# Rotary pairs fetched by four small DMA copies per tile, and a layer loop written out, in a two-layer streaming encoder

## The chip, the cores and the metric

One core of one Trainium2 chip runs the whole step. The metric is the device time of one execution in microseconds (us); of several runs the median is given. TensorE multiplies matrices, VectorE and ScalarE work elementwise, GpSimd (POOL) copies, fills and issues DMAs from its own queue, SyncE (SP) issues the weight DMAs.

## The reference

Two request groups (528 prompt frames with 16 meta tokens, 64 running frames, together 592) go through two layers. What touches the change, per layer:

```python
proj = rmsnorm(x, norm1_g) @ w_in
q, k, v, ... = split(proj)            # 16 query heads, 2 key/value heads of 64
q = partial_rotary(q, pos); k = partial_rotary(k, pos)

def partial_rotary(x, pos):           # ROT_DIM 16, half 8
    x1, x2 = x[..., :8], x[..., 8:16]
    return concat([x1*cos - x2*sin, x2*cos + x1*sin, x[..., 16:]])
```

Then follow sliding-window attention, a short convolution branch, a Conformer branch with a convolution of width 31, a gated merge with the output projection, and a ConvFFN. After the second layer comes a final RMSNorm.

## The kernel before

Data lie channel-major: 128 channels on the partitions, 592 frames (TOK) along the free axis, so the 1024 channels are eight tiles and a tile holds two query heads. A weight panel is 128 output channels by 1024 inputs; 174 panels (PANELS) per layer pass through two buffers. For a panel in buffer s, SP loads raw weights (L310), ScalarE makes the high part (`step`, L732), VectorE the low part (`step`, `low`, L982), and TensorE does 8 x 3 x 2 = 48 matmuls of 128x296 (`panel`, L424): high by high, high by low, low by high, two halves of the frames. When a panel is done, both `step`s prepare the panel after next.

The order of work on each engine is written out by hand, one program per engine, with semaphores between them; each engine takes its instructions in that order. Layers are a hardware loop with a register, `Fori(0, DEPTH)`, on GpSimd (L326), TensorE (L595), ScalarE (L776) and VectorE (L1066); inside a layer there are smaller hardware loops.

The Q stage works so. TensorE runs the K panel (L641), then eight Q panels (`queries`, L630), then V (L647). ScalarE copies each result from PSUM into one of two slots of a scratch area (K: L808, Q: L814, V: L817; the slots are O_QR). For the rotation TensorE multiplies the copied tile by a permutation matrix with signs (`rotate`, L612 with the matmul in L616, one Q panel later), and VectorE forms tile x cos (L1146), sin x product (L1148) and their sum (L1150). For the keys TensorE makes four such products (`keys`, L620, L626): each of the two key heads, plain and permuted, written to both halves of the partitions; VectorE multiplies them by cos and sin (L1135) and adds (L1138, L1139) into KD, which has each key head on both halves. Between the rotations VectorE works off convolution taps of the Conformer branch (`taps`, L1029; `first_taps`, L1017), and a `step` per panel. After the last rotation it does six taps, the step of V, and then the first score maxima of attention (L1188). GpSimd copies the rotated queries of a chunk into a padded staging area (`stage`, L345, L358, L359), for the first key head once four rotations are done, for the second once all eight are; TensorE's first scores (L499) need that, the copied V and the keys.

At the layer's turn TensorE begins with blocks of the first two panels (`two_panels`, L450), then a channel sum (L460); ScalarE takes the root (L751 loads the table, L753), VectorE the reciprocal (L1000).

Of the kernel before, what the change touches and what calls it, by code (L numbers as in the profile page):

```python
# [66 lines left out]
D_CF, D_K, D_Q, D_V, D_OA, D_SC, D_OS, D_OC, D_WO, D_FF, ND = 0, 8, 12, 20, 22, 30, 46, 54, 62, 70, 116  # L67
# [15 lines left out]
PIECES = ((0, 0, HALF, 0), (1, 0, TP - HALF, HALF), (1, TP - HALF, DEC_SEQ, TP))  # L83
# [68 lines left out]
def encoder(nc, weights, xt, vecs, consts, kcache, vcache, cfhist, spill, y, kp, vp, scp, cfp, ffp, ks, vs):  # L152
# [24 lines left out]
    nsink = sb("neg_sink", [128, DEPTH * 8])  # L177

# [48 lines left out]


# [26 lines left out]
    qrot_ps, krot_ps = sem("qrot_ps"), sem("krot_ps")  # L255
# [63 lines left out]
    def _(pool):  # L319
# [6 lines left out]
        with pool.Fori(0, DEPTH) as l:  # L326
# [16 lines left out]
            plain()  # L343

            def stage(c, n):  # L345
# [66 lines left out]
    def _(pe):  # L412
        def panel(w, s, out, nk, rh, rl, kwait=None, k0=0, k1=KT, between=None):

            pe.wait_ge(lo_done, w + 1)
            for k in range(k0, min(nk, k1)):
                if between and k == 2:
                    between()
# [3 lines left out]
                for j, (a, b) in enumerate(((wh, rh), (wh, rl), (wl, rh))):  # L422
                    for h in range(2):
                        last = nc.tensor.matmul(out[:, h, :], a[:, s, wk], b[:, k, h * HALF:(h + 1) * HALF],  # L424
                                                start=(k == 0 and j == 0), stop=(k == nk - 1 and j == 2))
# [3 lines left out]
        def two_panels(w, outs, nk, r0, r1, free, kwait, last_late, middle=None):  # L429
# [7 lines left out]
            order += [(p, k) for p in range(2) for k in range(nk - 3, nk)]  # L437
            for u, (p, k) in enumerate(order):
# [9 lines left out]
                for j, (a, b) in enumerate(((wh, rh), (wh, rl), (wl, rh))):  # L448
                    for h in range(2):
                        last = nc.tensor.matmul(outs[p][:, h, :], a[:, p, wk], b[:, k, h * HALF:(h + 1) * HALF],  # L450
# [17 lines left out]
        def residual(l, w, d, nk, rh, rl, kwait):  # L468

            two_panels(l * PANELS + w, (d_tile(d), d_tile(d + 1)), nk, (rh, rl), (rh, rl),  # L470
                       [(d_out, d_free(l, d + j)) for j in range(2)], kwait, True)
            with pe.Fori(1, 4) as i:
                for j in range(2):
                    pe.wait_ge(d_out, l * ND + i * 2 + (d + j + 1))
                    panel(l * PANELS + i * 2 + (w + j), j, d_tile(d + j), nk, rh, rl)

        def first_pair(l, w, a, d, kwait, last_late, middle=None):

            two_panels(w, (a_tile(a), d_tile(d)), KT, (xh, xl), (xh, xl), ((a_out, a_free(l, a)), (d_out, d_free(l, d))),
                       kwait, last_late, middle)  # L480

        def pair(l, w, a, d, rg, ro, kwait=None, middle=None):

            pe.wait_ge(a_out, a_free(l, a[0]))
            panel(w, 0, a_tile(a[1]), KT, *rg)
# [3 lines left out]
            panel(w + 1, 1, d_tile(d[1]), KT, *ro, kwait=kwait)  # L489
# [80 lines left out]
        def attention_end(l):  # L570
# [3 lines left out]
            def gate_part(k0, k1):  # L574
                panel(l * PANELS + P_OA, 0, a_tile(A_OA), KT, xh, xl, k0=k0, k1=k1)
# [19 lines left out]
        with pe.Fori(0, DEPTH) as l:  # L595
# [7 lines left out]
            def glu(i, j):  # L603
                pair(l, W + i * 4 + (P_CF + 2 * j), (i * 2 + (A_CF + j), A_CF + j), (i * 2 + (D_CF + j), D_CF + j),
                     (xh, xl), (xh, xl))
            first_pair(l, W + P_CF, A_CF, D_CF, (nx_lo, l * 24), False, mean_square1)
            first_pair(l, W + P_CF + 2, A_CF + 1, D_CF + 1, (nx_lo, l * 24 + 8), False)
# [4 lines left out]
            def rotate(i, j):  # L612
                pe.wait_ge(a_out, l * NA + i * 2 + (A_Q + j + 3))
                pe.wait_ge(d_out, l * ND + i * 2 + (D_Q + j + 1))
                for h in range(2):
                    last = nc.tensor.matmul(d_tile(D_Q + j)[:, h, :], con[:, CON["rot"]:CON["rot"] + 128],  # L616
                                            slot(O_QR, TOK, j)[:, h * HALF:(h + 1) * HALF], start=True, stop=True)
                last.then_inc(qrot_ps, 1)

            def keys():  # L620

                pe.wait_ge(a_out, a_ready(l, A_K))
                for j, name in enumerate(("ka", "kar", "kb", "kbr")):
                    pe.wait_ge(d_out, d_free(l, D_K + j))
# [974 lines left out]
```

## Time and profile before

| | |
|---|---|
| three runs | 2595.13, 2599.48, 2603.38 us, median 2599.48 |
| profiled execution | span 2596.4 us from the first to the last instruction; no other time of its own is given |
| TensorE (PE), weight loads (PEld) | busy 2533.4 us, 2493.8 us |
| VectorE, ScalarE, GpSimd | busy 1649.4, 865.6, 74.3 us |

Busy time is the union of an engine's instructions. Matmuls overlap in the records, so one lasts about 300 ns while a pair starts every 270 ns; the pace is read from starts. An idle time in square brackets names what ended it; "issue" means that nothing the profile shows was waited for.

### The profile page before, as it was taken

To read this page: it belongs to the slowest core of one execution; us is meant where nothing else is said; L and a number is where in the kernel's file an instruction comes from. 1 tells how busy PE (TensorE), PEld (TensorE's weight loads), DVE (VectorE), ACT (ScalarE), POOL (GpSimd) and SP (SyncE) were. 2 spreads that over 40 slices of the span, in tenths; PEclk is the share of its full clock that TensorE was granted. 3 is DMA by queue.
4 is the path that set the end of the run, shared out by engine and by line. 5 is a ranking of instruction groups with operands and counts; after the bars stand their busy time and mean duration, and the time that the engine had idled before them with its cause. 6 is when DMAs were issued, how large, how long until landed. Compare 5 with 4: busy or idle time off the path is not lost.

```text
span 2596.4 us, 49209 instructions
## 1 busy us (share of the span) xinstructions
PE 2533.4 (98%) x17938; PEld 2493.8 (96%) x17938; DVE 1649.4 (64%) x2468; ACT 865.6 (33%) x1624; POOL 74.3 (3%) x133
## 2 busy tenths in 40 slices
PE   6999999999999999999999999999999999999997
PEld 6998899999999999999999988999999999999996
DVE  8768667776534663645777775777755356546367
ACT  4124422223523442423432143322235234324244
POOL 0002100000000000000000021000000000000000
PEclk9998899999999999999999979999999999999998
DMA  4220012222233222222232100222222322222222
GB/s 180 81 65 25 8 65 81 80 77 79 82 105 95 75 80 81 81 81 81 94 106 81 65 9 8 81 82 81 81 74 87 104 91 82 78 79 79 81 81 104
DMA packets 55331, 203.13 MB, mean 78 GB/s; under 512 B 6606, under 2 KB 6670, under 8 KB 54958
## 3 DMA queue, kind: packets, MB, share of 16 engines
q1 hardware_dynamic: 52560, 190.03, 22.3%
q0 software_dynamic: 2656, 11.57, 1.5%
q8 instruction: 72, 1.18, 0.2%
q14 instruction: 43, 0.35, 0.0%
HBM read 193.14 MB, written 8.50 MB: 78 GB/s over the span
## 4 chain that ended last, share of the span: by engine, by line
PE 93%; DVE 3%; issue 2%; ACT 1%; DVEq 0%; DMA 0%; ACTq 0%; SPq 0%
PE ps L424 79%; PE ps L450 5%; PE ps L535 4%; PE ps L499 2%; PE ps L514 1%; PE ps L516 1%; DVE w_lo L982 1%; DVE cf_acc L1029 1%; ACT w_hi L732 0%; PE ps L547 0%; PE ps L460 0%; PE ps L616 0%; DVE scratch L996 0%; DVE x_q_merged L1458 0%; DMA vec<-in_vecs 0%
## 5 line engine op out<-in xcount | busy, mean ns | idle before, releaser
L424 PE MATMUL ps<-xn_hi,w_hi 128*128 128x296 f32 x3584 | 786.3, 301 | 4.8 <-DVE w_lo L982 4.7
L424 PE MATMUL ps<-xn_hi,w_lo 128*128 128x296 f32 x3584 | 781.5, 299 | 0.0
L424 PE MATMUL ps<-xn_lo,w_hi 128*128 128x296 f32 x3584 | 779.6, 299 | 0.0
L982 DVE TENSOR_TENSOR w_lo<-raw,w_hi 128x1024 fp32r<-128x1024 f32 x350 | 429.1, 1226 | 540.3 <-ACT w_hi L732 538.1
L732 ACT ACTIVATE w_hi<-raw 128x1024 fp32r<-128x1024 f32 x348 | 369.0, 1060 | 1205.9 <-PE ps L424 1141.2
L424 PEld LDWEIGHTS ps<-xn_hi,w_hi 128*128 128x128 f32 x3584 | 583.9, 189 | 8.0 <-DVE w_lo L982 5.8
L424 PEld LDWEIGHTS ps<-xn_lo,w_hi 128*128 128x128 f32 x3584 | 583.5, 189 | 0.0
L424 PEld LDWEIGHTS ps<-xn_hi,w_lo 128*128 128x128 f32 x3584 | 581.0, 188 | 0.0
L1029 DVE SCALAR_TENSOR_TENSOR cf_acc<-glu,vec,cf_acc 128x622 f32<-128x622 f32 x368 | 295.7, 862 | 0.1
L424 PE MATMUL ps<-branch_hi,w_hi 128*128 128x296 f32 x1296 | 284.0, 300 | 0.3
L424 PE MATMUL ps<-branch_hi,w_lo 128*128 128x296 f32 x1296 | 282.3, 299 | 0.0
L424 PE MATMUL ps<-branch_lo,w_hi 128*128 128x296 f32 x1296 | 281.6, 299 | 0.0
L424 PEld LDWEIGHTS ps<-branch_hi,w_hi 128*128 128x128 f32 x1296 | 210.6, 188 | 2.3 <-DVE w_lo L982 1.7
L424 PEld LDWEIGHTS ps<-branch_lo,w_hi 128*128 128x128 f32 x1296 | 210.8, 189 | 0.0
L424 PEld LDWEIGHTS ps<-branch_hi,w_lo 128*128 128x128 f32 x1296 | 209.8, 188 | 0.0
L1404 DVE SCALAR_TENSOR_TENSOR scratch<-scratch,vec 128x594 f32<-128x594 f32 x176 | 147.2, 837 | 54.4 <-ACT scratch L943 45.7
L943 ACT ACTIVATE scratch<-scratch,vec 128x594 f32<-128x594 f32 x88 | 69.9, 795 | 164.2 <-DVE scratch L1427 99.5
L1450 DVE TENSOR_TENSOR x_q_merged<-x_q_merged,ps 128x592 f32 x48 | 37.0, 771 | 128.3 <-PE ps L424 118.4
L1017 DVE SCALAR_TENSOR_TENSOR cf_acc<-glu,vec,cf_acc (+1 forms) x112 | 97.1, 867 | 27.5 <-DVE cf_acc L1017 20.5
L535 PEld LDWEIGHTS ps<-scratch 128*128 128x128 f32 (+3 forms) x576 | 89.6, 197 | 19.6 <-DVE scratch L1204 3.6
L535 PE MATMUL ps<-scratch 128*128 128x64 f32 (+5 forms) x576 | 105.0, 300 | 2.6 <-DVE scratch L1204 2.6
L499 PE MATMUL ps<-scratch 128*128 (+4 forms) x320 | 72.9, 387 | 7.4 <-ACT scratch L828 5.1
(159 smaller groups left out, 2325.0 us busy)
## 6 DMA issues: line engine op xcount, KB each, us to landing
raw<-in_weights SPq DMA_DIRECT2D x350, 512.0 KB, 3.3
spill<-x_q_merged POOLq DMA_DIRECT2D x2, 2368.0 KB, 9.7
x_q_merged<-spill POOLq DMA_DIRECT2D x16, 296.0 KB, 3.1
x_q_merged<-in_xt SPq DMA_DIRECT2D x4, 592.0 KB, 8.2
out_y<-x_q_merged SPq DMA_DIRECT2D x8, 296.0 KB, 2.3
con<-in_consts SPq DMA_DIRECT2D x1, 592.0 KB, 11.3
vec<-in_vecs SPq DMA_DIRECT2D x1, 576.0 KB, 5.7
out_cfp<-glu POOLq DMA_DIRECT2D x4, 120.0 KB, 5.6
```

The lines of the kernel that those rows point to most:

```text
L424: last = nc.tensor.matmul(out[:, h, :], a[:, s, wk], b[:, k, h * HALF:(h + 1) * HALF], start=(k == 0 and j == 0), stop=(k == nk - 1 and j ...
L450: last = nc.tensor.matmul(outs[p][:, h, :], a[:, p, wk], b[:, k, h * HALF:(h + 1) * HALF], start=(k == 0 and j == 0), stop=(k == nk - 1 an ...
L499: last = nc.tensor.matmul(PS[:, 2 * v + i // 2, 256 * (i % 2):256 * (i % 2) + nk], view(O_QS + 512 * v + 128 * i, 128), keys, start=True, ...
L514: last = nc.tensor.transpose(PS[0:n1, 4, 128 * i:128 * i + 128], P[:, 0:n1], ident)
L535: last = nc.tensor.matmul(PS[:, 6, 64 * i:64 * i + 64], scr[0:nn, o + 512 * v + 128 * i:o + 512 * v + 128 * i + 128], vals, start=(i == 0 ...
L732: nc.scalar.activation(wh[:, s, :], raw[:, s, :], ACT.Copy).then_inc(hi_done, 1)
L943: nc.scalar.activation(dst, src[:, 0:S_OUT], ACT.Identity, bias=0.0, scale=col(l, "ffw", m * 3)) \
L982: return V.tensor_tensor(wl[:, s, :], raw[:, s, :], f(wh[:, s, :]), ALU.subtract).then_inc(lo_done, 1)
L1017: V.scalar_tensor_tensor(tile(acc, m), src, col(l, "cfw", m * CF_K + k), tile(acc, m), ALU.mult, ALU.add).then_inc(tap_glu, 1)
L1029: V.scalar_tensor_tensor(a, tile(G, 2 * g + t, k, CF_OUT), col(l, "cfw", k + (2 * g + t) * CF_K), a, ALU.mult, ALU.add).then_inc(tap_rest[ ...
L1404: V.scalar_tensor_tensor(dst, src[:, k:k + S_OUT], col(l, "ffw", m * 3 + k), dst, ALU.mult, ALU.add) \
L1450: V.tensor_tensor(halves(tile(X, m)), halves(tile(X, m)), d_tile(d0 + n + j), ALU.add) \
```

## The change

- Rotation without TensorE: `rotate` and `keys` go, with their PSUM places. GpSimd issues four DMA copies per tile inside the scratch area (`partners`): for each of the two heads of a tile rows 8 to 15 to the place of rows 0 to 7, and back (8 rows of 592 floats each). VectorE multiplies by a sine whose sign is set once, in layer 0. The other partner rows are zeroed once per layer by GpSimd.
- Keys: K is rotated once, 128 partitions, as a tile; VectorE then writes the sum of each head to both halves.
- The copied K goes to slot 1 instead of 0; copies and issues wait for the rotation two tiles back.
- The layer loop is written out on the four engines: the layer number is a constant.
- The first kept frame of a layer becomes a function, `first(l)`, which is 0 for both layers; `kept`, `kept_tile`, `half(l)` and `pieces(first(l))` stand where the whole tile, HALF and PIECES stood (these many lines are left out below). After the last layer the casts for a next layer are left out.

```diff
+ROT_IN = 4 * 16
...
+KEEP0 = (0, 0)
+def first(l):
+    return KEEP0[min(l, DEPTH - 1)]
+def half(l):
+    return (TOK - first(l)) // 2
...
 @block.gpsimd
-        with pool.Fori(0, DEPTH) as l:
+        for l in range(DEPTH):
...
+            pool.wait_ge(glu_first, l + 1)
+            nc.gpsimd.memset(view(O_TQ, 2 * TOK), 0.0).then_inc(rot_zero, 1)
+            pool.wait_ge(rot_zero, l + 1)
+            def partners(s):
+                for h in (0, HEAD_DIM):
+                    x1, x2 = slice(h, h + ROT // 2), slice(h + ROT // 2, h + ROT)
+                    pool.dma_start(slot(O_TQ, TOK, s)[x1, :], slot(O_QR, TOK, s)[x2, :]).then_inc(rot_in[s], 16)
+                    pool.dma_start(slot(O_TQ, TOK, s)[x2, :], slot(O_QR, TOK, s)[x1, :]).then_inc(rot_in[s], 16)
+            pool.wait_ge(a_out, a_ready(l, A_K))
+            partners(1)
+            for m in range(KT):
+                pool.wait_ge(a_out, a_ready(l, A_Q + m))
+                pool.wait_ge(qrot, l * KT + m + 1)
+                if m == 1:
+                    pool.wait_ge(krot, l * 2 + 2)
+                partners(m % 2)
             def stage(c, n):
-                        pool.wait_ge(qrot, l * KT + 4 * (v + 1))
+                        pool.wait_ge(qrot, l * KT + (4 * (v + 1) + 2))
...
 @block.tensor
-        with pe.Fori(0, DEPTH) as l:
+        for l in range(DEPTH):
...
-            def rotate(i, j):
...
-            def keys():
...
                     panel(W + i * 2 + (P_Q + j), 1 - j, a_tile(A_Q + j, half(l)), KT, xh, xl)
-                    if j:
-                        rotate(i, 0)
-                    elif isinstance(i, int):
-                        keys()
-                    else:
-                        rotate(i - 1, 1)
...
-            panel(W + P_V, 1, a_tile(A_V), KT, xh, xl, between=lambda: rotate(3, 1))
+            panel(W + P_V, 1, a_tile(A_V), KT, xh, xl)
...
 @block.scalar
-                        nc.scalar.activation(tile(xh, i * 2 + j), tile(X, i * 2 + j), ACT.Identity, bias=0.0,
-                                             scale=col(squares[0], g, i * 2 + j)).then_inc(nx_hi, 1)
+                        if squares[0] < DEPTH:
+                            nc.scalar.activation(kept_tile(xh, i * 2 + j, l), kept_tile(X, i * 2 + j, l), ACT.Identity,
+                                                 bias=0.0, scale=col(squares[0], g, i * 2 + j)).then_inc(nx_hi, 1)
...
-        with act.Fori(0, DEPTH) as l:
+        for l in range(DEPTH):
...
-            nc.scalar.activation(halves(slot(O_QR, TOK, 0)), a_tile(A_K), ACT.Copy).then_inc(a_out, 1)
+            nc.scalar.activation(halves(slot(O_QR, TOK, 1)), a_tile(A_K), ACT.Copy).then_inc(a_out, 1)
...
-                    act.wait_ge(d_out, l * ND + i * 2 + (D_Q + j + 1))
-                    act.wait_ge(krot_ps, l * 4 + 4)
+                    act.wait_ge(qrot, l * KT + i * 2 + (j + 1))
+                    if j:
+                        act.wait_ge(krot, l * 2 + 2)
...
-            act.wait_ge(qrot, l * KT + (KT - 1))
+            act.wait_ge(qrot, l * KT + (KT + 1))
...
 @block.vector
+        V.sem_inc(qrot, 2)
...
-        with dve.Fori(0, DEPTH) as l:
+        for l in range(DEPTH):
...
+            if l == 0:
+                dve.wait_ge(late_in, 16)
+                dve.wait_ge(con_in, 16)
+                V.tensor_reduce(sign[:, :], con[:, CON["rot"]:CON["rot"] + 128], AX.X, ALU.add).then_inc(sign_done, 1)
+                dve.wait_ge(sign_done, 1)
+                V.tensor_scalar(sin, sin, sign[:, 0:1], -1.0, ALU.mult, ALU.mult).then_inc(sign_done, 1)
+                dve.wait_ge(sign_done, 2)
             def keys():
+                kc, kr = slot(O_QR, TOK, 1), slot(O_TQ, TOK, 1)
+                dve.wait_ge(rot_in[1], l * (5 * ROT_IN) + ROT_IN)
+                V.tensor_tensor(kc, kc, cos, ALU.mult).then_inc(kmul, 1)
+                V.tensor_tensor(kr, kr, sin, ALU.mult).then_inc(kmul, 1)
+                dve.wait_ge(kmul, l * 2 + 2)
                 for v in range(N_KV):
+                    r = slice(64 * v, 64 * v + 64)
+                    for o in (0, 64):
+                        V.tensor_tensor(KD[o:o + 64, v, 0:TP], kc[r, 0:TP], kr[r, 0:TP], ALU.add)
+                        last = V.tensor_tensor(KD[o:o + 64, v, TP + WINDOW:720], kc[r, TP:TOK], kr[r, TP:TOK], ALU.add)
+                    last.then_inc(krot, 1)
...
             def rotation(i, j):
-                V.tensor_tensor(tile(X, i * 2 + j), slot(O_QR, TOK, j), cos, ALU.mult).then_inc(qtmp, 1)
-                dve.wait_ge(qrot_ps, l * KT + i * 2 + (j + 1))
-                V.tensor_tensor(halves(slot(O_TQ, TOK, j)), halves(sin), d_tile(D_Q + j), ALU.mult).then_inc(d_out, 1)
-                dve.wait_ge(d_out, l * ND + i * 2 + (D_Q + j + 3))
-                V.tensor_tensor(tile(X, i * 2 + j), tile(X, i * 2 + j), slot(O_TQ, TOK, j), ALU.add).then_inc(qrot, 1)
+                V.tensor_tensor(kept_tile(X, i * 2 + j, l), kept(slot(O_QR, TOK, j), l), kept(cos, l), ALU.mult) \
+                    .then_inc(qtmp, 1)
+                dve.wait_ge(rot_in[j], l * ((4 + j) * ROT_IN) + i * ROT_IN + ((j + 1) * ROT_IN))
+                V.tensor_tensor(kept(slot(O_TQ, TOK, j), l), kept(slot(O_TQ, TOK, j), l), kept(sin, l), ALU.mult) \
+                    .then_inc(qtmp, 1)
+                dve.wait_ge(qtmp, l * (2 * KT) + i * 4 + (2 * j + 2))
+                V.tensor_tensor(kept_tile(X, i * 2 + j, l), kept_tile(X, i * 2 + j, l), kept(slot(O_TQ, TOK, j), l), ALU.add) \
+                    .then_inc(qrot, 1)
...
                         if final:
-                            scaled_lo(l + 1, "g1", m, (l + 1) * 24 + i * 2 + (j + 1))
+                            if l + 1 < DEPTH:
+                                scaled_lo(l + 1, "g1", m, (l + 1) * 24 + i * 2 + (j + 1))
```

## Rows read from the trace of the kernel before

**Rows 1.** The page: busy time by engine, and engines of the chain that ended last.
```profile
PE 2533.4 (98%) x17938; PEld 2493.8 (96%) x17938; DVE 1649.4 (64%) x2468; ACT 865.6 (33%) x1624; POOL 74.3 (3%) x133
...
PE 93%; DVE 3%; issue 2%; ACT 1%; DVEq 0%; DMA 0%; ACTq 0%; SPq 0%
```

**Rows 2.** Chain of waits, layer 0, 142 to 158 us: start us, us, what.
```profile
141.93 0.97 PE ps L424 x7
...
146.06 2.26 PE ps L626 x8
148.32 6.56 PE ps L424 x48
154.88 1.00 PE ps L616 x4
```

**Rows 3.** Instructions of lines 616 and 626, whole span: durations in ns, min/median/max.
```profile
L616 PE MATMUL ps<-scratch,con x64: 412/412/413, 154.7 to 1486.8; 128*128 128x296 f32 x64
...
L626 PE MATMUL ps<-scratch,con x32: 412/412/517, 142.7 to 1431.3; 128*128 128x296 f32 x32
```

**Rows 4.** Timeline of ScalarE, end of the Q stage: start us, us, engine, line, instruction.
```profile
200.32 1.06 ACT L732 ACTIVATE w_hi<-raw 128x1024 fp32r<-128x1024 f32 x1 [5.93 <-PE ps L424]
201.28 0.65 ACT L814 ACTIVATE scratch<-ps 128x592 f32<-128x592 f32 x1
```

**Rows 5.** Timeline of VectorE, Q stage of layer 0.
```profile
166.97 4.75 DVE L1029 SCALAR_TENSOR_TENSOR cf_acc<-glu,vec,cf_acc 128x622 f32<-128x622 f32 x6
...
201.85 1.22 DVE L982 TENSOR_TENSOR w_lo<-raw,w_hi 128x1024 fp32r<-128x1024 f32 x1
202.99 0.77 DVE L1146 TENSOR_TENSOR x_q_merged<-scratch,con 128x592 f32 x1
203.68 0.76 DVE L1148 TENSOR_TENSOR scratch<-con,ps 128x592 f32<-128x592 f32 x1
...
207.34 5.17 DVE L1029 SCALAR_TENSOR_TENSOR cf_acc<-glu,vec,cf_acc 128x622 f32<-128x622 f32 x6
...
213.77 0.21 DVE L1188 TENSOR_REDUCE score_max<-ps 128x4 f32<-128x64 f32 x1
```

**Rows 6.** Timeline of GpSimd: staging copies of layer 0, and a DMA issue.
```profile
207.66 0.79 POOL L358 COPY scratch<-x_q_merged 64x256 f32<-64x256 f32 x1 [23.55 <-DVE x_q_merged L1150]
...
212.83 1.27 POOL L358 COPY scratch<-x_q_merged 64x256 f32<-64x256 f32 x1
...
1296.99 0.54 POOL L332 DMA_DIRECT2D spill<-x_q_merged  x1 [38.22 <-DVE x_q_merged L1450]
```

**Rows 7.** DMA issues of GpSimd: KB each, median us from issue to landing.
```profile
out_cfp<-glu POOLq DMA_DIRECT2D x4, 120.0 KB, 5.6
...
glu<-in_cfhist POOLq DMA_DIRECT2D x2, 120.0 KB, 10.0
...
out_kp<-scratch POOLq DMA_DIRECT2D x4, 32.0 KB, 1.8
```

**Rows 8.** Timelines of VectorE, TensorE and ScalarE at the turn of the layer.
```profile
1295.55 0.77 DVE L1450 TENSOR_TENSOR x_q_merged<-x_q_merged,ps 128x592 f32 x1 [1.21 <-PE ps L424]
...
1306.60 0.26 DVE L1069 MEMSET glu<- 128x240 f32 x1 [7.43 <-issue]
...
1297.71 0.53 PE L450 MATMUL ps<-xn_hi,w_hi 128*128 128x296 f32 x2 [2.33 <-issue]
...
1315.65 0.70 PE L450 MATMUL ps<-xn_hi,w_hi 128*128 128x296 f32 x2 [2.06 <-DVE xn_lo L1079]
...
1299.77 1.28 ACT L751 ACT_TABLE_LOAD   x1 [1.83 <-issue]
```

**Rows 9.** Windows, turn and attention: busy us per engine, PEclk, DMA share, GB/s.
```profile
1296.00:1316.00 20.00, 16.23 (x102) 15.75 (x103) 12.15 (x13) 7.34 (x10) 1.45 (x2) 0.91 0.49 170
...
235.00:330.00 95.00, 93.71 (x524) 84.19 (x523) 62.53 (x143) 37.79 (x158) 16.91 (x31) 0.86 0.03 6
```

**Rows 10.** Timeline of ScalarE at the end of the run.
```profile
2583.24 0.75 ACT L753 ACTIVATE scratch<-ps,con 128x592 f32<-128x592 f32 x1 [0.82 <-PE ps L460]
```

More of the change, by code:

```diff
@@ L226, in a_piece, with kept, kept_tile @@
         return PS[:, 2 * (a % 2) + piece[0], piece[1]:piece[1] + piece[2]]
+    def kept(ap, l):
+        return ap[:, first(l):TOK]
+    def kept_tile(t, m, l):
+        return tile(t, m, first(l), TOK - first(l))
     raw_in = [sem("raw_in0"), sem("raw_in1")]
@@ L412, in _, with panel @@
     def _(pe):
-        def panel(w, s, out, nk, rh, rl, kwait=None, k0=0, k1=KT, between=None):
+        def panel(w, s, out, nk, rh, rl, kwait=None, k0=0, k1=KT):
+            n = out.shape[2]
+            t0 = TOK - 2 * n
             pe.wait_ge(lo_done, w + 1)
             for k in range(k0, min(nk, k1)):
-                if between and k == 2:
-                    between()
                 if kwait:
@@ L574, in gate_part @@
             def gate_part(k0, k1):
-                panel(l * PANELS + P_OA, 0, a_tile(A_OA), KT, xh, xl, k0=k0, k1=k1)
+                panel(l * PANELS + P_OA, 0, a_tile(A_OA, half(l)), KT, xh, xl, k0=k0, k1=k1)
             values(l, n - 1, n - 1, 1)
@@ L928, in _ @@
                     act.wait_ge(tails_out, l * 32 + 32)
-                    nc.scalar.activation(tile(mh, i * 2 + j), tile(X, i * 2 + j), ACT.Copy).then_inc(mg_hi, 1)
+                    nc.scalar.activation(kept_tile(mh, i * 2 + j, l), kept_tile(X, i * 2 + j, l), ACT.Copy).then_inc(mg_hi, 1)
             residual(l, P_WO, D_WO, (l, Q_N2), "g2")
-            root(l, S_N2, A_N2, HALF, O_RF)
+            root(l, S_N2, A_N2, half(l), O_RF + first(l))
             act.wait_ge(ff_zero, l * 4 + 4)
@@ L973, in _ @@
                 residual(l, p0 + 2 * n, d0 + n, (l + 1, Q_N1) if t0 + n == FT else None, "g1")
-        root(DEPTH, S_N1, A_N1, HALF, O_RT)
+        root(DEPTH, S_N1, A_N1, half(DEPTH), O_RT + first(DEPTH))
     @block.vector
@@ L1098, in _ @@
             dve.wait_ge(d_out, d_ready(l, D_CF))
-            for piece in PIECES:
+            for piece in pieces(0):
                 last = V.tensor_tensor(tile(G, 0, after(piece[3], CF_H), piece[2]),
@@ L1114, in glu @@
                 dve.wait_ge(a_out, l * NA + i * 2 + (A_CF + j + 3))
-                for piece in PIECES:
+                for piece in pieces(0):
                     last = V.tensor_tensor(tile(G, m, after(piece[3], CF_H), piece[2]),
@@ L1294, in _ @@
                     dve.wait_ge(a_out, l * NA + i * 2 + (A_SC + j + 3))
-                    for piece in PIECES:
+                    for piece in pieces(first(l)):
                         o = after(piece[3], S_H)
@@ L1305, in _ @@
                     bt = slot(O_BT, TOK, j)
-                    for piece in PIECES:
+                    for piece in pieces(first(l)):
                         o = piece[3] + (S_H if piece[3] >= TP else 0)
```

178 lines of the change are left out of this document (89 added, 89 removed).

## The prediction

> **What bounds the kernel now.** I read the busy shares first, then the chain of waits, then the timelines of the Q stage engine by engine. TensorE is busy 98% of the span and carries 93% of the chain that ended last [rows 1]; so time is won where a TensorE instruction goes away or an idle gap of TensorE closes, and lost where another engine makes it wait. In the Q stage (K, eight Q panels, V) the chain is TensorE panel after panel, 48 matmuls in 6.56 us each, with a rotation product of 1.00 us behind each Q panel, and after the first one a longer break for the keys [rows 2]. 64 records for the queries and 32 for the keys, over both layers, are all the work of that kind [rows 3].
>
> I count from T, the end of a Q panel on TensorE. The first ends at 141.93 + 0.97 = 142.90, and the next starts at 148.32, so the keys cost 5.42 us [rows 2]. ScalarE casts the next weights 0.12 us after a panel; 200.32 therefore puts the end of the eighth Q panel, T7, at 200.20 [rows 4].
>
> At the stage's end TensorE is not the limit. VectorE runs two rotations (202.99 to 207.34), six convolution taps, the weight step of V, and only then at 213.77 the first score maximum, T7 + 13.57 [rows 5]. Attention cannot start before that maximum.
>
> **What goes.** Before T7 stand the keys and six of the eight rotations (two per pair, the last two behind T7): 5.42 + 6 x 1.00 = 11.4 us per layer leave TensorE and move T7 forward by as much. The last two rotations, 2.0 us more, lie beside VectorE's chain to 213.77 and gain nothing by themselves.
>
> **What VectorE pays.** A rotation keeps three VectorE instructions, one now from SBUF instead of PSUM; both kinds last 0.77 us and start 0.69 to 0.8 apart [rows 5], so 2.2 us as before. Keys: four products and four adds become two products and eight adds of half the partitions; with the same row lengths this comes to about 5 us, as now, and the second Q cast needs it only 6.56 + 1.2 us after the first panel. Nothing. The sign product of layer 0 (two small instructions, about 1 us) lies ahead of the K step, beside TensorE's K panel; nothing, and at most 1 us if that cover were gone.
>
> But a pair of panels shrinks from 15.1 to 13.1 us, while VectorE's work in it stays: two steps at 1.14 (start to next start), two rotations at 2.2 and six taps, 4.75, in all 11.4 [rows 5]. It still fits, with a longer backlog at the end: sixth rotation and taps end at T6 + 1.2 + 1.14 + 2.2 + 4.7 = T7 + 2.6, instead of 201.85 = T7 + 1.65. From there step, two rotations, taps, V step as now (213.77 - 201.85 = 11.9): maximum at T7 + 14.6. That takes back 1.0 us.
>
> **What GpSimd adds.** Per tile it waits for ScalarE's copy, then issues four copies; 36 per layer, 72 in all, on its queue ahead of the query staging. ScalarE's copy ends at 201.93 = T7 + 1.73 [rows 4]. The first issue follows some 0.7 us later: the spill copy started at 1296.99, its releaser on VectorE ended at 1295.55 + 0.77 = 1296.32 [rows 6, 8]. Four at 0.54 each [rows 6] run from T + 2.4 to T + 4.6, the last starting at T + 4.0. Landing: nearest row 1.8 us, a small copy issued by the same engine; farther 5.6, farthest 10.0 [rows 7]. I take 1.8, for 8 rows of 2.4 KB are small too: landed at T + 5.8. VectorE reads the partners of tiles 0 to 6 only after the next panel's step, T + 6.56 + 1.2 + 1.14 + 0.7 = T + 9.6: hidden, with 3.8 us spare. Tile 7 has no panel between: its second product could start at T7 + 2.6 + 1.14 + 2.2 + 0.7 = T7 + 6.6. Hidden by 0.8 only. If each issue lasted as long as the GpSimd copy that VectorE slowed, 1.27 [rows 6], it would land 2.2 us later, 1.4 late; with a landing of 5.6 it is 3.0 late; together 5.2 per layer. Below nothing is excluded: a wait cannot be earlier than the data.
>
> The Trainium skill (SBUF — State Buffer, section on the two separate sides) says that VectorE in a two-port mode locks GpSimd out of the port through which it writes descriptors. If that held beside rotations and taps, the issue would go by the upper price just given, 2.8 us over two layers and 2579 us.
>
> The query staging for the second key head, two copies that wait for the last rotation, already slows the taps now (5.17 instead of 4.75). The staging for the first head now comes after the last four issues and lands beside the rotations too: 0.4 us more, by the same difference. The zeroing of the partner slots reads nothing and runs in the GLU stage; nothing, up to 1.2 us in layer 1, where VectorE is briefly the limit.
>
> Per layer: 11.4 - 1.0 - 0.4 = 10.0; I keep 9.8 for the waits that the counts round off. Two layers: **19.6 us**.
>
> **The layer loop.** The diff also unrolls it on four engines. At the jump back TensorE stands 2.33 us with nothing to wait for, ScalarE 1.83, VectorE 7.43 [rows 8]. In the 20 us from there the granted clock is 0.91 on average [rows 9], that is 0.09 / 0.5 x 20 = 3.6 us at 1.2 GHz instead of 2.4, half of it lost, 1.8. With no jump, the first matmul blocks end 2.33 + 1.8 = 4.1 us earlier, the square sum, root and reciprocal follow them, and the wait for xn_lo at 1315.65 moves with TensorE's panels and stays as long. I take **4.0 us**; bounds 0 (the code fetch comes anyway) and 5.9 (ScalarE's 1.83 counts as well).
>
> **The rest.** In the last layer eight casts and eight subtractions go; at the tail ScalarE waits for the channel sum by 0.82 us [rows 10], so they were off the path: nothing. All "kept" slices start at 0 (KEEP0 is zero twice): the same sizes. Wait values without a layer register save sequencer work only where an engine is not waiting; I give nothing.
>
> Sum: 19.6 + 4.0 = 23.6. The profiled execution spans 2596.4 us, the median of the runs is 2599.48, 3.1 more for what lies around it and for spread; the page gives no separate time for that execution. 2599.5 - 23.6 = **2576 us**.
>
> **Rivals.**
> - *Partners late at tile 7 alone.* 1.4 to 5.2 us per layer given back: 2579 to 2586. For it: a margin of 0.8 us, bursts of weights on the same engines. Against: 1.8 in the near row. Chance 0.15.
> - *The code fetch is paid anyway*, in straight code instead of at the jump: 2580. For it: the fetched code grows. Against: no other TensorE gap without a releaser in the span. By the Trainium skill (Advanced Engine Details and Errata, ISA Cache) most engines hold only two lines of 256 instructions; straight code is then fetched throughout as well, and no run here has shown yet at what price. Chance 0.10.
> - *The clock in attention.* There TensorE is the limit and gets 0.86 of its clock on average, stretches of 1.2 GHz between stretches of 2.4 [rows 9]. A later or earlier start may shift how they fall. From 0.86 to 0.82 is 95 x 0.86 / 0.82 - 95 = 4.6 us per layer, 2585; as much the other way, 2567. Against: the work in it is unchanged. Chance 0.08 for the bad side.
> - *Slower: every tile waits for its copies.* With the farthest landing, 10.0, partners come at T + 14.0, 4.4 us after VectorE wants them. VectorE runs its steps, rotations and taps in order, so the step behind the wait is late: a pair costs 11.4 + 4.4 = 15.8 instead of 13.1, 2.7 x 3.5 pairs = 9.5 us, and tile 7 waits 7.4: 16.9 per layer against 9.8 won, 7.1 lost, twice, less 4.0: 2610. It decides from a landing of about 9 us, where both terms reach 11.8. Against: that row is a copy of 128 partitions in many short pieces issued behind a large one. Chance 0.07.
>
> The forecast keeps 0.60. A measurement of this kernel can tell about 0.3%, 7.8 us. Faster by more (under 2591.7): forecast, the fetch rival, most of the first and part of the clock: 0.82. Within: 0.11. Slower: 0.07. The range runs from the good side of the clock with the best case of the jump, 2576 - 9.2 - 1.9 = 2565, to where late partners meet the bad clock in one layer, 2586 + 4.6, rounded to 2591; beyond it lie the slow rival and some of the mixtures.
>
> **What would show it.** Right: no rotation or key product on TensorE; consecutive Q panels 6.56 us apart; first maximum near T7 + 14.6 in both layers; no TensorE gap without a releaser at the layer's turn; partner copies landing within 2 us of issue. Wrong: VectorE waiting for a copy ahead of a step, TensorE waiting for w_lo between Q panels, issues of 1 us or more, a pause in straight code, or an attention stretch whose mean clock leaves 0.86.

## The result, and the profile after

The changed kernel takes 2575.16 us (median of four runs, 2571.93 to 2577.56) against 2601.43 for the kernel before in the same comparison: a ratio of 0.990, with a 95% interval of 0.988 to 0.992. Measured again beside its two halves it took 2578.70 against 2600.75, ratio 0.992 (0.991 to 0.993). The two gains are 26 and 22 us; the forecast was 23.6, 2576 us. The profiled execution lasted 2571.93 us, its span 2570.8, so 25.6 less than the span of before.

The page of the changed kernel, answering to [rows 1]:

```profile
PE 2512.2 (98%) x17842; PEld 2478.5 (96%) x17842; DVE 1644.4 (64%) x2466; ACT 859.2 (33%) x1616; POOL 114.6 (4%) x207
...
PE 94%; DVE 4%; ACT 1%; issue 1%; DMA 0%; POOL 0%; DVEq 0%; ACTq 0%; SPq 0%; POOLq 0%
```

TensorE has 96 instructions fewer, the 64 and 32 of [rows 3]. The kernel is still bound by TensorE; "issue" in the chain, idle time without a releaser, is down from 2% to 1%.

The chain of waits from the Q stage into attention in layer 0 of the changed kernel (start us, us, what), where [rows 2] had a break between panels:

```profile
119.96 67.11 PE ps L473 x491
...
189.40 0.52 POOL scratch L381
...
191.16 3.43 DMA scratch<-scratch
194.60 0.02 issue
194.62 0.79 DVE scratch L1191
...
196.12 5.45 DVE cf_acc L1062 x6
201.57 1.34 DVE w_lo L1014
...
203.96 2.33 DVE scratch L1224 x5
...
206.33 1.02 PE ps L567 x4
```

Line 473 is now the panel (424 before). The panels run on without a break to T7 = 187.06; then the chain leaves TensorE: it goes through the partner copies of the eighth tile, the last rotation, the taps, V's weight step, the first maximum. No other tile's copies are in it.

ScalarE's casts put the ends of the first and the eighth Q panel 0.12 us ahead of these two rows, the second of which answers to the first of [rows 4]:

```profile
141.26 1.06 ACT L761 ACTIVATE w_hi<-raw 128x1024 fp32r<-128x1024 f32 x1 [5.03 <-PE ps L473]
...
187.18 1.06 ACT L761 ACTIVATE w_hi<-raw 128x1024 fp32r<-128x1024 f32 x1 [4.95 <-PE ps L473]
...
203.51 0.20 ACT L856 ACTIVATE sink_exp<-sink_diff 128x4 f32<-128x4 f32 x1 [6.73 <-PE ps L687]
```

From first to eighth panel it is 45.92 us; before it was 200.32 - 143.01 = 57.31 by the same casts, [rows 4] and this one of the kernel before:

```profile
143.01 1.06 ACT L732 ACTIVATE w_hi<-raw 128x1024 fp32r<-128x1024 f32 x1 [4.96 <-PE ps L424]
```

The third of the rows above is the first exponential. It waits for two things, TensorE's transposes of the values (line 687) and VectorE's chain from the first maximum to line 1240. The brackets name the transposes, but these end at 202.62 and line 1240 ends at 203.43 (both below), so VectorE came last.

VectorE, GpSimd and TensorE from T7 on in the changed kernel (timelines; answering to [rows 5, 6]):

```profile
189.40 0.52 POOL L381 DMA_DIRECT2D scratch<-scratch  x1 [4.51 <-ACT scratch L845]
...
189.70 1.22 DVE L1014 TENSOR_TENSOR w_lo<-raw,w_hi 128x1024 fp32r<-128x1024 f32 x1
...
192.32 0.85 DVE L1194 TENSOR_TENSOR x_q_merged<-x_q_merged,scratch 128x592 f32 x1
192.58 0.85 POOL L408 COPY scratch<-x_q_merged 64x256 f32<-64x256 f32 x1
193.10 0.97 DVE L1188 TENSOR_TENSOR x_q_merged<-scratch,con 128x592 f32<-128x592 f32 x1
...
194.62 0.78 DVE L1191 TENSOR_TENSOR scratch<-scratch,con 128x592 f32<-128x592 f32 x1 [0.56 <-DMA scratch<-scratch]
...
198.22 1.38 PE L552 MATMUL ps<-scratch 128*128 128x16 f32 x8 [2.78 <-POOL scratch L408]
...
199.44 3.18 PE L687 MATMUL ps<-con,scratch 128*128 128x128 f32 x15
...
202.83 0.21 DVE L1233 TENSOR_REDUCE score_max<-ps 128x4 f32<-128x64 f32 x1
...
203.27 0.16 DVE L1240 TENSOR_TENSOR sink_diff<-neg_max,neg_sink 128x4 f32<-128x4 f32 x1
```

The step of the eighth panel starts at T7 + 2.64, the first maximum at T7 + 15.77, where [rows 5] had T7 + 13.57. VectorE waits 0.56 us for the partners (0.28 in layer 1). TensorE waits 2.78 us for the staging of the second key head (line 408).

The turn of the layer in the changed kernel, answering to [rows 8] (ScalarE, VectorE):

```profile
1284.40 1.06 ACT L761 ACTIVATE w_hi<-raw 128x1024 fp32r<-128x1024 f32 x1 [2.46 <-PE ps L473]
...
1296.32 1.06 ACT L761 ACTIVATE w_hi<-raw 128x1024 fp32r<-128x1024 f32 x1 [5.79 <-PE ps L502]
...
1288.14 0.26 DVE L1103 MEMSET glu<- 128x240 f32 x1
```

The pauses are gone: the memset that had stood behind 7.43 us follows its predecessor at once. Between the two casts lie 11.92 us, where the kernel before had 1311.26 - 1295.42 = 15.84:

```profile
1295.42 1.06 ACT L732 ACTIVATE w_hi<-raw 128x1024 fp32r<-128x1024 f32 x1 [2.39 <-PE ps L424]
...
1311.26 1.06 ACT L732 ACTIVATE w_hi<-raw 128x1024 fp32r<-128x1024 f32 x1 [5.88 <-PE ps L450]
```

So the 25.6 us of the two profiles come apart, cast by cast, as follows (less is negative): start-up until the K panel -1.8; from the first to the eighth Q panel -11.4 in each layer; from there to the first panel behind attention +2.0 and +1.5; turn of the layer up to the next K panel -5.4; all the rest +0.9. The sum is -25.6.

### The profile page after: what moved, and what is told of

Same layout as the page of the kernel before. It is cut to its first block, busy times and chain, and to the rows that moved or that the text cites. A ratio compares the mean times of both kernels' runs of the same rounds, so it can differ in the third digit from the quotient of the medians.

```text
span 2570.8 us, 47457 instructions
## 1 busy us (share of the span) xinstructions
PE 2512.2 (98%) x17842; PEld 2478.5 (96%) x17842; DVE 1644.4 (64%) x2466; ACT 859.2 (33%) x1616; POOL 114.6 (4%) x207
## 4 chain that ended last, share of the span: by engine, by line
PE 94%; DVE 4%; ACT 1%; issue 1%; DMA 0%; POOL 0%; DVEq 0%; ACTq 0%; SPq 0%; POOLq 0%
PE ps L473 81%; PE ps L502 5%; PE ps L588 4%; PE ps L552 2%; PE ps L567 1%; PE ps L569 1%; DVE w_lo L1014 1%; DVE cf_acc L1062 0%; PE ps L600 0%; ACT w_hi L761 0%; PE ps L513 0%; DMA scratch<-scratch 0%; DVE xn_lo L1113 0%; DVE scratch L1028 0%; DVE x_q_merged L1509 0%
## 5 line engine op out<-in xcount | busy, mean ns | idle before, releaser
L588 PEld LDWEIGHTS ps<-scratch 128*128 128x128 f32 (+3 forms) x576 | 88.5, 194 | 19.6 <-issue 2.6
## 6 DMA issues: line engine op xcount, KB each, us to landing
scratch<-scratch POOLq DMA_DIRECT2D x72, 18.5 KB, 2.8
```

The lines of the kernel that those rows point to most:

```text
L588: last = nc.tensor.matmul(PS[:, 6, 64 * i:64 * i + 64], scr[0:nn, o + 512 * v + 128 * i:o + 512 * v + 128 * i + 128], vals, start=(i == 0 ...
```

## The experiments

For each kernel the table gives four lengths of its profiled execution, all from ScalarE's weight casts: first to eighth Q panel, eighth Q panel to the first panel behind attention ("attention", layers 0 and 1), last panel of layer 0 to the first of layer 1 ("turn"). "Long passes" are those of attention's passes, from one start of the transpose of chunk results (line 600 in the changed kernel) to the next, that last over 6.5 us (the last few of a layer also carry blocks of a weight panel); the section on the hardware shows why they matter.

| kernel | Q panels | attention | long passes | turn | median us | ratio to before (95%) |
|---|---|---|---|---|---|---|
| before | 57.3 / 57.3 | 138.6 / 138.6 | 6 / 6 | 15.84 | 2601.4 | |
| changed | 45.9 / 45.9 | 140.6 / 140.1 | 7 / 7 | 11.92 | 2575.2 | 0.990 (0.988 to 0.992) |
| loop alone | 57.4 / 57.4 | 140.5 / 139.4 | 8 / 8 | 11.92 | 2597.4 | 0.999 (0.997 to 1.000) |
| rotary alone | 45.9 / 45.9 | 142.2 / 138.7 | 7 / 7 | 14.57 | 2581.3 | 0.993 (0.992 to 0.995) |
| tile 7 without copies | 45.9 / 45.9 | 140.7 / 137.5 | 8 / 7 | 11.92 | 2574.9 | 0.991 (0.989 to 0.992) |
| taps first | 45.9 / 45.9 | 141.4 / 140.7 | 9 / 7 | 11.93 | 2575.0 | 0.991 (0.990 to 0.992) |
| eight copies | 45.9 / 45.8 | 147.4 / 145.3 | 10 / 11 | 11.92 | 2582.3 | 0.992 (0.990 to 0.995) |
| sixteen copies | 52.6 / 52.6 | 151.2 / 155.3 | 8 / 9 | 11.92 | 2614.5 | 1.006 (1.004 to 1.008) |
| values first | 45.9 / 45.9 | 136.9 / 130.4 | 7 / 6 | 11.93 | 2562.9 | 0.986 (0.984 to 0.988) |
| values alone | 45.9 / 45.9 | 139.7 / 139.6 | 6 / 7 | 11.93 | 2576.1 | 0.992 (0.990 to 0.994) |
| before, values first | 57.3 / 57.3 | 145.2 / 136.1 | 9 / 7 | 14.37 | 2602.6 | 1.001 (1.000 to 1.002) |
| changed again | 45.9 / 45.9 | 142.0 / 140.8 | 7 / 7 | 11.93 | 2578.7 | 0.992 (0.991 to 0.993) |
| rotary again | 45.9 / 45.9 | 144.2 / 141.2 | 8 / 7 | 15.87 | 2584.2 | 0.993 (0.992 to 0.995) |
| loop again | 57.4 / 57.4 | 135.1 / 138.6 | 5 / 7 | 11.93 | 2595.2 | 0.998 (0.997 to 0.999) |

### The two halves of the change

The loop alone is the kernel before with this edit on GpSimd, TensorE, ScalarE and VectorE:

```diff
-        with pe.Fori(0, DEPTH) as l:
+        for l in range(DEPTH):
```

> The kernel before with nothing changed but its layer loop, written out on four engines; the rotation products stay on TensorE. My theory: the pauses without a releaser at the turn of the layer go (2.33 us on TensorE, 1.83 on ScalarE, 7.43 on VectorE) and the turn gives 4.0 to 5.9 us; with the 1.8 us by which the changed kernel was already early ahead of its first Q stage, if these belong to the loop too, up to 7.5: 2592 to 2596 us against 2600. Rival, the fetch is paid anyway in straight code: within 1 us of before, and a pause without a releaser somewhere behind the turn. Rival, the early 1.8 us belong to another part or to that one execution: 5.4 and no more, with the first Q panel ending at 142.9 as before.

The rotary edit alone is the changed kernel with the four loops put back; the sign is then worked out in both layers, into a column per layer, and the last layer's casts and subtractions are back:

```diff
-        for l in range(DEPTH):
+        with pe.Fori(0, DEPTH) as l:
...
-                V.tensor_scalar(sin, sin, sign[:, 0:1], -1.0, ALU.mult, ALU.mult).then_inc(sign_done, 1)
+            V.tensor_scalar(sin, sin, sign[:, bass.ds(l, 1)], -1.0, ALU.mult, ALU.mult).then_inc(sign_done, 1)
```

> The changed kernel with its layer loop kept as a hardware loop, so the rotary edit alone. My theory: 9.5 us less per layer from the first Q panel's end to the first transpose of the probabilities, 19 in all, 2581 us against 2600; first Q panel's end to the eighth's 45.9 us in both layers, partner copies needed late at tile 7 alone, by about 0.5 us; the three pauses at the turn of the layer are back. Rival, the two parts are not independent (straight code also frees GpSimd's and VectorE's sequencers in the Q stage): 15 or less, 2585 and above. Rival, the rotary edit carries the early 1.8 us as well: 21, 2579.

Measured: 2597.38 us, ratio 0.999, and 2581.32 us, ratio 0.993, against 2598.91 for the kernel before in the same comparison. By the ratios the loop gave 3.6 us (-0.5 to 7.8), less than its text expected, and the rotary edit 17.2 (12.5 to 22.1). The turn of the layer with the loop alone, by ScalarE's casts:

```profile
1299.84 1.06 ACT L732 ACTIVATE w_hi<-raw 128x1024 fp32r<-128x1024 f32 x1 [2.46 <-PE ps L424]
1311.76 1.06 ACT L732 ACTIVATE w_hi<-raw 128x1024 fp32r<-128x1024 f32 x1 [5.79 <-PE ps L450]
```

and with the rotary edit alone (VectorE, ScalarE):

```profile
1299.27 0.26 DVE L1103 MEMSET glu<- 128x240 f32 x1 [7.44 <-issue]
...
1292.30 1.28 ACT L780 ACT_TABLE_LOAD   x1 [1.71 <-issue]
```

The written-out loop gives a turn of 11.92 us in the one kernel as in the other, and the hardware loop brings the pauses back. But the turn of the rotary edit alone is 14.57 us and not 15.84. TensorE stands still about as long there, 2.57 us against 2.33. (The profile ends this pause with VectorE's low part of the weights; the written-out code has the same waits and no such pause.) What differs is the clock. The windows of the turn from cast to cast, in the kernel before and with the rotary edit alone (busy us of TensorE, weight loads, VectorE, ScalarE and GpSimd, PEclk, the granted clock as a share of 2.4 GHz, DMA share, GB/s):

```profile
1295.42:1311.26 15.84, 13.54 (x85) 13.31 (x85) 8.06 (x7) 4.67 (x6) 1.45 (x2) 0.89 0.58 209
```
```profile
1288.08:1302.65 14.57, 12.04 (x85) 11.81 (x86) 6.81 (x6) 4.68 (x6) 1.45 (x2) 1.00 0.62 226
```

So the pause is worth some 2.5 us in each execution with the hardware loop, and the lower clock behind it 1.4 more in two of the four (15.84 and 15.87 in the table, against 14.57 and 14.37).

The rival that the fetch is paid elsewhere falls: the profile of the loop alone has no pause of over 0.5 us without a releaser on TensorE in the whole span. The early 1.8 us belong to neither half: the K panel's cast starts at 136.44 in the kernel before, 134.62 in the changed one, 138.22 with the loop alone, 136.44 with the rotary edit alone. It is scatter of the start-up.

By the ratios the halves together gave 20.8 us (the next text reckons with 2.6 for the loop, and so with 19.8) and the whole 26.8, so all three were measured once more, on one chip:

> The changed kernel once more, beside its two halves on one chip. What is open: the loop alone gave 2.6 us and the rotary edit alone 17.2, 19.8 together, while both gave 26.8. My theory: the two are independent, 4 and 20, and what is missing is the scatter of attention's clock: this run 24 us under the kernel before, 2575. Rival, they help one another: 26 or more here with the halves as they were.

> The rotary edit alone once more. My theory, independent parts: 19 to 20 us under the kernel before, 2580, 4 above the changed kernel. Rival, the edits help one another: 17 or less, 8 or more above the changed kernel.

> The written-out loop alone once more. My theory: 4 us under the kernel before. Rival, the turn's 4 us are lost again in attention: 1 us or less.

Measured: 2578.70, 2584.16 and 2595.17 us against 2600.75, that is 22.1, 16.6 and 5.6 us by medians, or by the ratios 21.1, 17.9 and 6.0. The halves now add up to 24 and the whole is 21. The parts are independent as far as these runs can tell. Over both rounds the ratios put the loop at 3.6 and 6.0 us and the rotary edit at 17.2 and 17.9.

### The late partners

The eighth tile without its copies leaves out that tile's rotation partners (its second product takes what the slot held):

```diff
-                partners(m % 2)
+                if m < KT - 1:
+                    partners(m % 2)
...
-                dve.wait_ge(rot_in[1], l * (5 * ROT_IN) + ROT_IN)
+                dve.wait_ge(rot_in[1], l * (4 * ROT_IN) + ROT_IN)
```

> The changed kernel without the four partner copies of the eighth query tile in each layer: that tile's second product takes what its slot held before, so its rotation is left out of the computation. My theory: the late partners at tile 7 cost their measured wait and little more, 0.56 us per layer, and GpSimd's queue is 2.1 us shorter ahead of the query staging: the first maximum 0.6 to 1.0 us earlier, 1 to 2 us in all, 2573 to 2574. Rival, the whole 0.8 us by which the maximum came later than my sum lies in slowed rotations and taps: 0 to 0.5 us. Rival, the late tile costs more further on: 2 us per layer and above, 2571 or less.

Measured: 2574.89 us, not to be told from the changed kernel. The trace says more: VectorE's wait is gone and the maximum starts at 203.64, with the eighth cast at 188.64, that is T7 + 15.12 instead of 15.77; in layer 1 it moves by 0.28, the wait there. So of the 1.2 us by which the maximum missed my T7 + 14.6 in layer 0 a little over half is the wait for the partners. The rest stays with the copies gone, in instructions that last longer where GpSimd's staging copies run beside them (0.85 and 0.97 us for VectorE's products of 0.77, 5.45 for taps of 4.75).

Each copy split by columns into two, then four, the same bytes:

```diff
+                    for t in range(0, TOK, TOK // 2):
+                        c = slice(t, t + TOK // 2)
-                    pool.dma_start(slot(O_TQ, TOK, s)[x1, :], slot(O_QR, TOK, s)[x2, :]).then_inc(rot_in[s], 16)
+                        pool.dma_start(slot(O_TQ, TOK, s)[x1, c], slot(O_QR, TOK, s)[x2, c]).then_inc(rot_in[s], 16)
...
-ROT_IN = 4 * 16
+ROT_IN = 8 * 16
```

> The changed kernel with each of the four partner copies split into two halves of the columns, eight issues per tile, the same bytes. My theory: 4 x 0.52 = 2.1 us more of issue per tile; tiles 0 to 6 are still covered (last landing about T + 9.0 against T + 9.6 needed), tile 7 waits 2.6 us instead of 0.56, which delays the staging of the second key head and the first maximum by 2.1: about 2 us per layer, 2579. Rival, the margin of tiles 0 to 6 is smaller than I reckoned: VectorE also waits there and the eighth Q panel comes later than 45.9 us behind the first; 2583 and above. Rival, attention's clock swallows it: within 1 us of the changed kernel.

> The changed kernel with each partner copy split into four quarters of the columns, sixteen issues per tile, the same bytes. By my reckoning GpSimd's queue is then the limit of the Q stage: a hop of 0.7 us and 16 x 0.52 us of issue, 9.0 us per tile against 6.56 for a Q panel; over the keys and eight queries the last landing falls about 24 us later per layer, and VectorE's steps behind the waits leave TensorE without weights: 48 us more, about 2620 us and slower than the kernel before. Rival, issue overlaps more than that (the copies of the next tile are prepared early): under 2600.

Measured: 2582.29 and 2614.45 us. Landings of the partner copies (KB each, median us from issue), in the changed kernel, with eight and with sixteen copies:

```profile
scratch<-scratch POOLq DMA_DIRECT2D x72, 18.5 KB, 2.8
```
```profile
scratch<-scratch POOLq DMA_DIRECT2D x144, 9.2 KB, 2.3
```
```profile
scratch<-scratch POOLq DMA_DIRECT2D x288, 4.6 KB, 1.6
```

VectorE's waits for them (us in total, times, longest), with eight and with sixteen:

```profile
DVE scratch L1193 <- DMA scratch<-scratch: 2.9, 2, 1.6
```
```profile
DVE scratch L1193 <- DMA scratch<-scratch: 41.3, 8, 5.8
...
DVE scratch L1176 <- DMA scratch<-scratch: 8.0, 2, 4.0
```

With eight copies only tile 7 waits, 1.56 and 1.35 us in the two layers instead of 0.56 and 0.28: tiles 0 to 6 have the spare time that I gave them, and the halves land sooner than the wholes, so the wait grows by 1.0 and not 2.1. The first maximum is only 0.7 and 0.8 us later than in the changed kernel; the other 6.0 and 4.3 us of the longer attention go along with ten and eleven long passes instead of seven. That the clock and not the copies made them so is likely, but only argued.

With sixteen copies GpSimd is the limit, as reckoned: the Q panels take 52.6 us, the first maximum starts 26.4 us behind the eighth cast, and the kernel is slower than before, 2614 against the 2620 that I expected. This is the slower rival of the prediction, brought about by issues rather than landings.

### What attention waits for

Taps first does each group of six taps one pair of panels earlier:

```diff
-                    taps(l, i + (TAPS_GLU - 1), 0, 1, 2)
+                    taps(l, i + TAPS_GLU, 0, 1, 2)
...
             V.sem_inc(carrier, 1)
+            taps(l, TAPS_GLU, 0, 1, 2)
...
-            taps(l, TAPS_GLU + 3, 0, 1, 2)
```

> The changed kernel with each group of six convolution taps in the Q stage done one pair of panels earlier, so that the last group no longer stands between the eighth rotation and the first score maximum; the work is the same. My theory, that VectorE's queue at the stage's end sets the start of attention: the maximum comes up to 5.45 us earlier, until the staging of the second key head (two GpSimd copies behind the eighth rotation) is the limit, 4 us per layer, 2567 us. Rival, TensorE waits for that staging anyway (2.8 us is its longest wait in the first scores): 1 to 2 us per layer, 2572. Rival, slower: the first group now stands in the pair that also rotates the keys, VectorE falls behind there and TensorE waits for weights: 2578 and above.

Measured: 2574.98 us, nothing won. Timelines of that kernel:

```profile
197.34 0.22 DVE L1233 TENSOR_REDUCE score_max<-ps 128x4 f32<-128x64 f32 x1
...
198.18 1.89 PE L552 MATMUL ps<-scratch 128*128 128x16 f32 x8 [2.74 <-POOL scratch L408]
...
199.91 3.44 PE L687 MATMUL ps<-con,scratch 128*128 128x128 f32 x15
...
203.38 0.20 ACT L856 ACTIVATE sink_exp<-sink_diff 128x4 f32<-128x4 f32 x1 [6.60 <-PE ps L687]
```

The maximum starts 5.5 us earlier, the first exponential 0.13 us earlier. ScalarE waits for the value transposes, these stand behind the scores of the second head, and those wait for its staging. The transposes end at 203.35, 0.7 us later than in the changed kernel, for TensorE's scores of the second head took 1.89 us instead of 1.38 and the transposes 3.44 instead of 3.18. Two waits that end within a microsecond of each other had held attention; taking one away leaves the other.

Values first takes both away: the edit above, and

```diff
-            attention(l, 0)
+            scores(l, 0, 0, 0)
             for j in range(2):
...
                 last.then_inc(vt_ps, 1)
+            scores(l, 0, 0, 1)
...
-            step(W, P_V, 1)
...
-            attention(0)
+            maxima(0, 0)
             value_tiles()
+            maxima(0, 1)
+            step(W, P_V, 1)
```

> The kernel with the taps done one pair earlier, and in addition the value transposes put ahead of the second key head's first scores on TensorE, the copies of the values between the two first maxima on VectorE, and V's weight step behind them. My theory: with the taps gone from there ScalarE's first exponentials wait for the transposes alone, which wait behind the scores of the second head; moved ahead of it, the exponentials start about 4.5 us earlier (11.7 us behind the eighth Q cast instead of 16.2) and the first turn of chunk 0 about 4 us earlier than in the run with the taps moved alone. If attention keeps its length from there, 8 us less than the changed kernel, 2567. Rival, attention's chunks at the lower clock take it back: the start is earlier, and the end of attention is not, 2572 to 2575.

Values alone is the second edit without the first.

> The changed kernel with the same reordering of value transposes, value copies and V's step, and the taps left where they were. My theory: VectorE's six taps still stand ahead of the first maximum, so only V's step, 1.4 us, and the 0.4 us by which the transposes end later than the maximum can be won: 1 to 2 us per layer, 2572 to 2574. Rival, TensorE's order was the whole limit: as much as in the other run. Rival, nothing, 2575.

Measured: 2562.92 us, ratio 0.986, the fastest kernel of the study, and 2576.13 for the second edit alone. Timelines of values first (eighth cast at 187.87):

```profile
195.98 1.83 PE L687 MATMUL ps<-con,scratch 128*128 128x128 f32 x15
...
196.78 0.22 DVE L1233 TENSOR_REDUCE score_max<-ps 128x4 f32<-128x64 f32 x1
...
197.85 0.20 ACT L857 ACTIVATE sink_exp<-sink_diff 128x4 f32<-128x4 f32 x1 [0.38 <-PE ps L687]
...
200.15 0.60 PE L567 MATMUL ps<-con,scratch 128*16 128x128 f32 x4
```

The exponentials start 10.0 us behind the eighth cast (16.3 in the changed kernel) and the first transposes of the probabilities, line 567, 12.3 (19.1). With the second edit alone the transposes are done at 198.64, but the maximum still stands behind VectorE's taps, 14.3 us behind the eighth cast:

```profile
202.97 0.21 DVE L1233 TENSOR_REDUCE score_max<-ps 128x4 f32<-128x64 f32 x1
```

Either edit alone gains nothing that can be told. Both together gain 12 us on the changed kernel's median and 13 on the second edit alone, which ran in the same comparison. That is more than the 8 expected, and the attentions, 3.7 and 9.7 us shorter, do not get it in equal parts.

The same two edits on the kernel before:

> The kernel before (rotation products on TensorE, hardware loop for the layers) with the same reordering that gave 2563 us on the changed kernel: taps one pair earlier, value transposes ahead of the second head's scores, V's step behind the first maxima. My theory: the reordering needs VectorE to have room in the Q stage, 15.1 us per pair of panels there against 13.1 in the changed kernel, so it serves as well as there: the first maximum about 6 us earlier, 6 us per layer at most, 2588 us; the gain is independent of the rotary edit. Rival: in the kernel before VectorE's chain at the stage's end is not what holds attention up (the rotation product of tile 7 and V's panel are), 2 us per layer or less, 2595 and above. Rival: attention's chunks at the lower clock take it back, 2598 to 2600.

Measured: 2602.61 us, ratio 1.001. The first maximum starts 2.8 us earlier behind the eighth panel, not 6, since it now waits for TensorE's scores. These start 9.6 us behind the eighth cast, 7.2 in the changed kernel, where the last two rotation products no longer stand ahead of them. The exponentials wait for the transposes behind the scores and win only 0.6 us in layer 0 and 1.8 in layer 1, against 6.4 and 6.1 on the changed kernel (layer 0, eighth cast at 202.33):

```profile
216.13 0.20 ACT L826 ACTIVATE sink_exp<-sink_diff 128x4 f32<-128x4 f32 x1 [2.20 <-PE ps L658]
```

So the theory failed at the start already: the reordering wins less here because of the rotation products, and the two edits are not independent. Attention is then 145.2 and 136.1 us long against 138.6: in layer 0, with nine long passes instead of six, more was lost behind the start than had been won, as the last rival has it, and in layer 1 the gain was kept. What makes the passes long in one layer and not in the other is open.

## Why the prediction was right

**What goes** is confirmed to a tenth: 11.4 us per layer forecast, 57.31 - 45.92 = 11.4 measured, in both layers and in each kernel with the rotary edit and four copies. Keys, sign and zeroing cost TensorE nothing: the eight panels follow one another at 6.56 us with no wait for weights.

**The backlog at the stage's end** was the right mechanism, too small in size. Up to the eighth panel's step it holds (T7 + 2.6 forecast, 2.64 measured). Behind that I had the maximum at T7 + 14.6, plus 0.4 for the staging, 15.0; it starts at 15.77 in layer 0, and in layer 1, 15.38 us behind the cast, at 15.5. The step that failed is the landing of the partner copies: I took 1.8 us from copies to memory [rows 7], they need 2.8 in the median and the last of tile 7 about 3.4, so the spare 0.8 us became a wait of 0.56 (0.28 in layer 1). A landing within 2 us was one of my signs of being right, and it did not come. The rival of the late partners is thus what happens, at a price below its lower end of 1.4. Issue times were right: first at T7 + 2.34, 0.52 us each.

A GpSimd issue slowed beside VectorE was the upper price of that rival. It did not come: all 72 issues last 0.52 to 0.55 us, those of tile 7 too, which run beside VectorE's step and products. The Trainium skill (SBUF — State Buffer, "SBUF: two separate sides") has GpSimd locked out of its descriptor writes while VectorE is in a two-port mode; no issue of this trace shows that, and whether the products run in such a mode here no trace tells. Halving and quartering the 18.5 KB of a copy takes the median landing from 2.8 us to 2.3 and 1.6. The Trainium skill (SBUF — State Buffer, "The DMA setup-cost knee") puts a transfer at a roughly fixed 2 us plus its bytes; the measured landings differ from that.

**"Attention cannot start before that maximum"** is true and no longer the whole. In the kernel before VectorE came last by 1.0 us (its chain to the exponentials ends at 214.57, the value transposes at 213.53). In the changed one the transposes, behind a 2.78 us wait for the second head's staging and 3.18 us long instead of 1.84, end 0.8 us ahead of VectorE's chain in layer 0 and 0.1 us in layer 1. I had named the staging as a cost to the taps, not as a wait of TensorE. From T7 to the end of attention the changed kernel gives back 2.0 and 1.5 us, against 1.4 forecast.

**The loop**: 4.0 forecast, 3.92 from last panel to first panel measured between the two profiles; 3.6 and 6.0 us by the ratios of the loop alone, the first of them not clear of nothing. Both terms of the sum are there, the pause of 2.33 us and 1.8 for the lower clock behind it, but the second is partly luck: of four executions with the hardware loop two had the lower clock, and in the others the turn is only 2.5 us longer than written out. That the K panel of layer 1 comes 5.4 us earlier has its other 1.5 in the GLU stage. Its length varies between executions of one kernel (107.1 and 108.6 us with the loop alone), and here the mean clock in it was the same before and after, 0.97, so the cause is open. The rival of the fetch in straight code falls: TensorE shows no pause without a releaser there, and the instruction queues in the profile carried 68 and 33 packets after, 72 and 43 before.

**The clock in attention** was the unsteady term that I gave 0.08: its mean over the stage went from 0.85 to 0.84 and 0.83. It did not decide the sign. Executions of one kernel differ by it, and attention's length with it (138.7 to 144.2 us over the two profiles of the rotary edit alone).

The sum came out right, 23.6 against 22 and 26. The rotary edit was overstated (19.6 against some 17.5) and the loop perhaps understated (4.0 against 3.6 and 6.0), both within what the runs can tell.

## What to carry to other kernels

In this kernel, work taken out of a stage that feeds a serial hand-over was gained only as far as the engines behind the hand-over had room. So reckon each queue's backlog at the stage's end, then look for the second wait that ends beside the first. When an edit at such a place gains nothing, take the next waiter away too before giving it up; here two edits gave nothing each and 12 us together. Copies of a few rows issued per tile are cheap while the next panel covers them, and the last tile has no next panel.

## What was not expected of the hardware

Attention runs in passes of two lengths. Starts of successive transposes of chunk results in the changed kernel, and the windows of one long and one short pass (columns as in the windows of the turn):

```profile
250.94 0.63 PE L600 MATMUL ps<-con,scratch 128*128 128x128 f32 x2
257.97 0.63 PE L600 MATMUL ps<-con,scratch 128*128 128x128 f32 x2
...
290.38 0.38 PE L600 MATMUL ps<-con,scratch 128*128 128x128 f32 x2
295.63 0.38 PE L600 MATMUL ps<-con,scratch 128*128 128x128 f32 x2
```
```profile
250.94:257.97 7.03, 7.03 (x35) 6.39 (x35) 4.44 (x10) 2.57 (x11) 0.79 (x2) 0.74 0.01 2
290.38:295.63 5.25, 5.25 (x36) 4.71 (x35) 4.65 (x11) 2.57 (x11) 3.35 (x7) 1.00 0.05 13
```

The same work takes 5.25 us at 2.4 GHz and 7.03 where the granted clock falls to 1.2 GHz for half of the pass. Between 5 and 11 of the 18 passes per layer are long, in most profiles not the same number in the two layers, and each long one costs 1.8 us. That is likely why changes of 1 us per layer can't be told in the medians.

The clock is also low behind TensorE's wait in the hand-over. The 15 value transposes take 1.83 us in values first and 3.18 in the changed kernel, behind a pause of 2.78 us; the windows of the two:

```profile
195.90:197.90 2.00, 1.91 (x18) 1.62 (x17) 1.90 (x6) 1.59 (x4) 0.80 (x2) 1.00 0.00 0
```
```profile
199.40:202.70 3.30, 3.22 (x16) 2.68 (x16) 3.30 (x4) 0.00 (x0) 2.33 (x3) 0.57 0.00 0
```

In all 16 layers whose TensorE waits 1.66 us or more for the second head's staging ahead of them (eight profiles, two layers each) these transposes take 3.1 to 3.4 us. In the 12 layers without that wait they take 1.84 us in ten, and 2.55 and 3.12 in the other two. So this wait was paid twice, 2.78 us of standing and 1.35 us of slower work behind it, but it is not all that brings the lower clock. Which history of TensorE sets the number of long passes later in the stage was not found out.
